# The down projection of an encoder layer: products one by one, and the weights of three of them made ahead

## The reference

```python
def swiglu(h, w_gu, w_down):
    gu = h @ w_gu
    gate, up = jnp.split(gu, 2, axis=-1)
    return (jax.nn.silu(gate) * up) @ w_down

def reference(x, ...):
    for l in range(DEPTH):                      # DEPTH = 2
        ...
        h = rms_norm(x, ffn_norm[l])
        x = x + swiglu(h, w_gu[l], w_down[l])
```

## Time and profile before

| | us |
|---|---|
| median of 3 runs (2769.6 to 2775.0) | 2771.93 |
| the profiled execution | 2774.79 |
| its span, first to last instruction | 2773.1 |
| layer 1: down projection, first to last start of a matmul | 1170.08 to 1387.59 |
| layer 2: the same | 2538.91 to 2756.43 |

### The profile page before, as it was taken

How to read it: one execution, slowest core, us unless ns; L and a number is a source line. 1 busy time by engine, 2 the same in 40 slices (tenths; PEclk the granted TensorE clock), 3 DMA queues, 4 the chain that set the end, 5 groups by cost and what they waited for, 6 DMA issues and landing times. The chain is left out here.

```text
span 2773.1 us, 37893 instructions
## 1 busy us (share of the span) xinstructions
PE 2623.2 (95%) x12976; PEld 2166.9 (78%) x12976; DVE 1706.1 (62%) x3334; ACT 1065.6 (38%) x2098; POOL 562.0 (20%) x521
## 2 busy tenths in 40 slices
PE   5999999989799999999979999999897999999997
PEld 5877788777588888878878778878785888888786
DVE  4277657663555555589943766666717555556897
ACT  3222655553522222334342226555515322223342
POOL 2000221110044544300000003111001545442000
PEclk9999999999999999999999999999999999999999
DMA  5211610004122221432232116000222222216123
GB/s 165 79 42 38 146 45 13 18 13 137 61 84 79 89 84 46 142 155 76 76 120 70 39 39 155 28 18 12 88 62 76 91 77 92 76 46 233 51 92 118
DMA packets 230942, 219.84 MB, mean 79 GB/s; under 512 B 54768, under 2 KB 191984, under 8 KB 230768
## 3 DMA queue, kind: packets, MB, share of 16 engines
q1 hardware_dynamic: 222864, 217.61, 24.7%
q10 hardware_dynamic: 7904, 0.04, 0.2%
HBM read 171.87 MB, written 45.73 MB: 78 GB/s over the span
## 5 line engine op out<-in xcount | busy, mean ns | idle before, releaser
L1984 PE MATMUL psum<-OPH_t,WH 128*128 128x512 f32 x704 | 274.5, 390 | 6.7 <-DVE WL L1529 4.8
L1984 PE MATMUL psum<-OPH_t,WL 128*128 128x512 f32 x704 | 273.9, 389 | 0.0
L1984 PE MATMUL psum<-OPL_t,WH 128*128 128x512 f32 x704 | 273.9, 389 | 0.0
L1529 DVE TENSOR_TENSOR WL<-RAW,WH 128x512 fp32r<-128x512 f32 x132 | 160.9, 1219 | 157.0 <-ACT WH L1073 157.0
L958 ACT ACTIVATE T<-T,G 128x192 f32<-128x192 f32 (+4 forms) x352 | 177.3, 504 | 195.4 <-DVE G L1282 191.7
L1792 PE MATMUL psum<-BH,AH 128*128 128x512 f32 x616 | 243.2, 395 | 8.1 <-DVE BL L1597 7.6
L1794 PE MATMUL psum<-BH,AL 128*128 128x512 f32 x616 | 242.4, 394 | 0.0
L1793 PE MATMUL psum<-BL,AH 128*128 128x512 f32 x616 | 242.0, 393 | 0.0
L1984 PE MATMUL psum<-OPH_b,WH 128*128 128x512 f32 x528 | 209.6, 397 | 15.4 <-ACT P1S L1113 9.8
L1882 PE MATMUL psum<-QK,QS 128*128 (+5 forms) x576 | 214.9, 464 | 1.5 <-DVE G L1282 1.5
L1418 DVE COPY PT<-psum 128x256 f32<-128x256 f32 (+3 forms) x254 | 105.5, 415 | 177.9 <-PE psum L1898 176.8
(11 more groups left out here) (193 smaller groups left out, 5668.5 us busy)
## 6 DMA issues: line engine op xcount, KB each, us to landing
RAW<-in_w_gu SPq DMA_DIRECT2D x176, 256.0 KB, 3.8
WDS<-in_w_down SPq DMA_DIRECT2D x88, 256.0 KB, 2.6
UR<-in_w_in SPq DMA_DIRECT2D x56, 256.0 KB, 3.2
g_mid<-GRES SPq DMA_DIRECT2D x28, 512.0 KB, 2.6
WDK<-in_w_down SPq DMA_DIRECT2D x44, 256.0 KB, 6.5
x_res<-X SPq DMA_DIRECT2D x2, 4096.0 KB, 13.7
PR<-in_w_out SPq DMA_DIRECT2D x32, 256.0 KB, 4.2
X<-x_res SPq DMA_DIRECT2D x2, 4096.0 KB, 14.4
```

The source lines that it names most:

```text
L1529: v.tensor_tensor(WL[i][:, :, :], w_source(i, j), WH[i][:, :, :].bitcast(F32), ALU.subtract).then_inc(w_lo, 1)
L1984: last = t.matmul(dst[:, :], w[i][:, k, :], h[o][:, k, :], start=(i in (1, 5, 6) and k == 0 and part == 0), stop=(i in (2, 3, 4) and k == ...
```

## The change

- The seven products run one after the other, in the order 3, 4, 1, 7, 6, 5, 2. In this order consecutive products need few new blocks of gated tiles, and these are fetched as halves (256 KB) when they are needed.
- Products 7 and 6 are accumulated onto the banks of 4 and 1 (no `start` on their first matmul) after those have been added to one target block. X is touched by 40 adds a layer, not 48.
- High and low parts of the weights of products 2, 5 and 7 (33 tiles) are made beside gate/up: SP loads raw tiles (RAWD), POOL makes the sum for product 7 (`part_added`), ACT the high part (`part_high`), DVE the low part (`part_low`), SP sends the pair to DRAM (`w_parts`, 512 KB each). One of them belongs to every fourth product of ORDER. In the down projection the pair is loaded into BR (which holds high and low weights now), three steps ahead. The other four products make their weights in the down projection as before.
- Four gated tiles are kept and 18 sent, not 8 and 14. POOL's list mixes the sums of weights and the gated tiles in another way; SP's list is tied to ORDER.
- `add_product(m)` stands four steps behind the last step of its product; X comes in four pieces of 1 MB.

The core of the diff:

```diff
-            STEPS = [(m, k) for k in range(NK) for m in (2, 5)] + [(m, k) for m in (1, 3, 4, 7, 6) for k in range(NK)]
-            RUNS = [2, 5, 1, 3, 4, 7, 6]
+            RUNS = [3, 4, 1, 7, 6, 5, 2]
+            STEPS = [(m, k) for m in RUNS for k in range(NK)]
+            PARTS = (2, 5, 7)
+            for q in range(len(PARTS) * NK):
+                MADE_BESIDE[16 + 4 * q].append(q)
...
+                    if i == 6:
...
+                        sp.wait_ge(product, DONE[6, NCH - 1])
+                        for k in range(4):
+                            kept_weights(k, 1)
+                        for k in (2, 3):
+                            g_back_in(k, (0, 0))
+                    elif i == 5:
+                        sp.wait_ge(product, DONE[5, NCH - 1])
+                        for k in range(4, 8):
+                            kept_weights(k, 1)
+                    elif i == 2:
+                        sp.wait_ge(product, DONE[2, NCH - 1])
+                        for k in range(8, NK):
+                            kept_weights(k, 1)
+                        for n_ in range(4):
+                            passing_weights(n_)
+                        g_back_in(4, (0, 0))
...
                 sp.wait_ge(g_s, 2 * NCH)
...
+                for n in range(4, len(STEPS)):
                     m, k = STEPS[n]
+                    if n in PASSING:
+                        passing_weights(n)
+                    elif m in PARTS:
+                        sp.wait_ge(step_s, n - 3)
+                        q = 3 * k + PARTS.index(m)
+                        sp.dma_start(BR[:, n % 4, :, :].bitcast(F32), w_parts[q]).then_inc(b_in[n % 4], 16)
+                    if n in (5, 7, 9, 11):
+                        sp.dma_start(X[:, n - 5:n - 3, :], x_res[:, n - 5:n - 3, :]).then_inc(x_again, 16)
+                    if m == 3 and k >= 4:
+                        g_back_in(k, (1, 1))
...
+                def part_low(q):
+
+                    dve.wait_ge(part_hi, q + 1)
+                    v.tensor_tensor(BP[:, q % 2, 1, :], part_source(q), BP[:, q % 2, 0, :].bitcast(F32),
+                                    ALU.subtract).then_inc(part_lo, 1)
...
-                    for m in RUNS[1:]:
-                        if n == LAST_STEP[m] + 3:
+                    for m in RUNS[:-1]:
+                        if n == LAST_STEP[m] + 4:
+                            if m == RUNS[0]:
+                                dve.wait_ge(x_again, 64)
                             add_product(m)
-                add_product(6)
+                add_product(RUNS[-1])
...
                         last = three(bank[BANKS[m][sub]][:, :], AH[:, n % 4, P * sub:P * sub + P], AL[:, n % 4, P * sub:P * sub + P],
-                                     BH[:, n % 4, :], BL[:, n % 4, :], k == 0, k == NK - 1)
+                                     BR[:, n % 4, 0, :], BR[:, n % 4, 1, :], k == 0 and m not in (6, 7),
+                                     k == NK - 1 and m not in (1, 4), skip=True)
```

More of the change, by code:

```diff
@@ new lines, in build_program, with raw_part, part_source @@
+            A_SUMS = running([bool(M[m][0][1]) for m, k in STEPS])
+            B_MADE = running([m not in PARTS for m, k in STEPS])
+            B_SUMS = B_MADE
+            B_LOADED = {n: sum(1 for o in range(n % 4, n + 1, 4) if o not in B_MADE) for n in range(len(STEPS)) if n not in B_MADE}
+            PASSING = sorted(B_SUMS, key=int)
+            PASSING = [n for n in PASSING if STEPS[n][0] != 1]
+            def raw_part(at_):
+                return RAWD[:, at_[0], at_[1], :]
+            def part_source(q):
+                first, sign, second = M[PARTS[q % 3]][1]
+                return BP[:, q % 2, 1, :].bitcast(F32) if sign else raw_part(first)
@@ L620, in g_tile, with g_ready @@
             def g_tile(j, half):
-                t = GRES[:, j % G_KEPT, :] if j >= G_SENT else GLA[:, j, :] if j < 5 else GLB[:, j - 5, :] if j < 13 else GLC[:, 0, :]
+                t = GRES[:, j % G_KEPT, :] if j >= G_SENT else GL[j][:, :]
                 return t[:, 512 * half:512 * half + 512]
+            def g_ready(eng, k, at_):
+                tile_, half = at_
+                if k < 2:
+                    eng.wait_ge(g_s, 2 * PAIRS[k][tile_] + half + 1)
+                else:
+                    eng.wait_ge(g_got[2 * tile_ + half][(k - 2) // 3], 48)
@@ L1643, in _ @@
                         sum_c12(j)
+                    for q in MADE_BESIDE[n - 1]:
+                        part_low(q)
                 step_sum(2)
@@ L1745, in _, with part_added, weight_sums @@
                         mean_powers(fam, b, plan[-1][0]["Q"] + 6)
-                def weight_sums(j):
-                    pool.wait_ge(raw_in[j % 2], 64 * (j // 2 + 1))
+                def part_added(q):
+                    if q % 3 < 2:
+                        return
+                    first, sign, second = M[PARTS[q % 3]][1]
+                    pool.wait_ge(rawd_in, 32 * (q // 3 + 1))
+                    if q >= 2:
+                        pool.wait_ge(part_out[q % 2], 16 * (q // 2))
+                    g.tensor_tensor(BP[:, q % 2, 1, :].bitcast(F32), raw_part(first), raw_part(second), ALU.add).then_inc(part_sum, 1)
+                def weight_sums(j, which=(5, 6, 7, 3)):
+                    if 5 in which:
+                        pool.wait_ge(raw_in[j % 2], 64 * (j // 2 + 1))
                     g0, g1 = RAW[:, j % 2, 0, 0:4, :], RAW[:, j % 2, 0, 4:8, :]
@@ L1753, in weight_sums @@
                                                  (7, g0, u0, ALU.subtract), (3, g1, WS[6][:, :, :], ALU.subtract)):
+                        if i not in which:
+                            continue
                         if j:
```

232 lines of the change are left out of this document (137 added, 95 removed), and 2 rows, old and new, of the table M.

## The result

The changed kernel takes **2784.95 us** (median of 6 runs, 2781.72 to 2789.7) and the kernel before 2772.09 (6 runs): a ratio of 1.0044, 95% interval 1.0031 to 1.0058. It is slower by 12.9 us. The profiled execution of it took 2786.61 us, its span 2784.9. T is again the end of gate/up: 1166.98 in layer 1 of this trace.

The account below looks back on a forecast made before the run. PE bounds gate/up, DVE's adds a stretch of down. Per layer 11.8 us lost at down's start, 8.3 gained, 2.4 tail: net +5.9, +11.8 in both; against the 2771.93 median 2784 us, range 2770 to 2797.

Parts of the forecast that it names:

- Gate/up, 0: Gate/up: making the weights beside it costs 0, bounds 0 to 2 us a layer, because PE sets the pace.
- The 8.3 us at the end of the interleaved products: Down projection: 8.3 us a layer lost while DVE adds finished products; running them one after the other regains it all.
- Tail, +2.4 a layer: End of each layer: eight adds instead of four behind the last matmul, 2.4 us a layer more.
- Step 0, 2.4: First down step: waits for its passing weight tile p0, landing 0.2 us after gate/up ends; 2.4 us lost (1.6 to 3.0).
- Steps 1 and 2, 0.4: Second and third down steps: DVE's nine operations take 5.8 us against PE's 5.4; 0.4 us lost.
- 9 x 0.60: Steps 1 and 2 of down: nine DVE operations at 0.60 us each, plus 0.4, make 5.8 us.
- Step 3, 7.0: Fourth down step: waits for step 4's passing tile p4, 38th load unit, through DVE's list order; 7.0 us lost (5.5 to 8.5).
- The clock, 2.0: Behind step 3's gap in down: PE restarts at half clock, costing 2.0 us more (1.5 to 2.4).
- the queue is quicker: Rival, start of down: loads run at 402 GB/s from the first issue, 6.2 us lost at step 3; about 2776 us; chance 0.18.
- the making isn't covered: Rival, gate/up: each of 33 weight makings holds PE for one DVE operation, 23 us a layer, 2830 us; chance 0.05.
- p4 not behind the backlog: Rival, start of down: step 4's passing tile lands within 9 us of gate/up's end; 2760 to 2765 us; chance 0.09.
- from step 4 on I take 0: Down from step 4: two steps' loads need 5.2 us of 5.4, helped by step 3's gap; 0 us lost.

Follow-up runs that it names:

- e4: Changed kernel with the making of ready weights beside gate/up left out except for the first pair of tiles; 2785.05 us.
- e11: Kernel before the change, with products 2 and 5 run in sequence instead of interleaved, product 2 added six steps later; no ready weights; 2758.2 us.
- e9: e8 with the first four passing weight tiles of product 6 issued earlier, at steps 22 to 25; 2756.87 us.
- e3: Changed kernel with products in the order 3, 4, 2, 7, 1, 5, 6, so the last goes to one tile (four adds, not eight); 2781.77 us.
- e8: e7 with the product order of e10 (3, 1, 2, 6, 4, 5, 7); 2764.63 us.
- e12: e9 with GpSimd multiplying the last gated tile at once again, not after step 3; 2759.66 us.
- e1: Changed kernel with 13 load units of 256 KB moved behind the passing tile of step 4, X issued three steps later; 2792.03 us.
- e6: Changed kernel with 6 load units of 256 KB, not 13, moved behind the passing tile of step 4; 2783.66 us.
- e10: Changed kernel with only the product order exchanged, for 3, 1, 2, 6, 4, 5, 7, and gated-half loads to suit; 2787.45 us.
- e5: e1 with SP's wait for the last gated tile moved from ahead of step 4's loads to step 8's; 2787.14 us.
- e7: Changed kernel with loads in the order the steps need them and GpSimd's last gated-tile multiplications held until after step 3; 2781.2 us.
- e2: Changed kernel with, in steps 3 to 10, DVE's low halves placed ahead of the sum for the next step; 2784.83 us.

## Why the prediction was right, point by point

The forecast, 2784 us, was made for the reasons that the trace shows: the late passing tile, the sum's place in DVE's list, the half clock and the longer tail. That the sum comes within 0.4 us of the loss in either layer is in part luck. Step 0 came out 1.2 to 1.4 us under its term, steps 1 and 2 1.6 over, step 3 1.4 under, the rest 0.6 to 1.5 over. And the largest term is no simple price.

- *Gate/up, 0:* right (377.90 and 378.00 us; e4).
- *The 8.3 us at the end of the interleaved products:* regained in full. e11 shows that sequence alone gives back 6.2 of them, without ready weights and without the new order. That ready weights buy nothing beyond them is borne out by e11, which is as fast as e9 without any; the changed kernel without them was not run.
- *Tail, +2.4 a layer:* 19.10 against 16.67 us; e3, e8 to e12 end in 16.6 to 16.7.
- *Step 0, 2.4:* too much for this trace. 1.0 and 1.2 us were lost. p0, the 14th unit, landed at T - 1.2 and not T + 0.2, so the count taken from the earlier trace rows was 1.4 us late. In the seven other kernels with the same list up to p0 (e1 to e6, e10) the loss is 0.7 to 2.4 us: this term varies from run to run.
- *Steps 1 and 2, 0.4:* too little; 2.0 were lost. The step that failed is "9 x 0.60": it took DVE's operations at the spacing that they have in the earlier trace rows, where GpSimd does nothing. Two of them took 1.7 us beside its multiplications. The sign was there: in the earlier trace rows a subtraction of the same size takes 1.27 us on average in gate/up, where GpSimd is busy for half the time, and the kernel before has low halves of 0.93 and 1.53 us at this very place.
- *Step 3, 7.0:* 5.6 were lost. p4 came at T + 15.1, forecast T + 16.0, and steps 1 and 2 had used up more of the time. Step 3 started at T + 17.2, forecast T + 18.0. e6 gives 0.6 us a unit (3.5 to 3.9 for six), so its cause, the 38th place in the queue, is shown.
- *The clock, 2.0:* what remains of the loss in the two layers, 3.5 and 2.6 us, is the half clock and small pauses. In layer 1, 13 matmuls, and in layer 2, 6 start about 0.43 us apart, 2.6 and 1.2 us more than at full clock, behind the same gap of 5.8 us.

Lost in all, it was 12.1 and 11.4 for a forecast 11.8. Of the rivals, "the queue is quicker" would have needed p4 at T + 12.4, and "the making isn't covered" gaps in gate/up; neither is there. "p4 not behind the backlog" named the point where that gap ends, T + 9.1, but not what follows: in e1 and e5, where the gap is gone, the loss comes later, and no kernel with this order came near its 2760 to 2765. The weak step is "from step 4 on I take 0": by e1, e5 and e6 it held only because the gap at step 3 gave the queue time, as the prediction itself says and did not follow up.

What stays open: why e5 loses as much as it does. From 1174 to 1182 its queue moved only 259 GB/s, while SP's list stood behind the four slots of WDS; more slots were not tried. e8 against e7, which differ in the order alone, shows that what comes second is the cause of the gaps from T + 39 on, and of what its steps need only the passing tiles become fewer: the gated halves are as many, and DVE has four operations a step and not three. Whether they cost by their bytes or by SP's waits for their slots is not shown.

## What to carry to other kernels

When a stage begins with a backlog of loads, count for each step what has to be there by then, not only what stands ahead of the first late tile: taking a load out of the way of one step helps only if the steps behind it can wait for it. A gap may be the time in which a queue catches up, and then removing it moves the loss. Before adding made-ahead operands and a new order, try the smallest edit on the stall that the trace shows: here running two products in sequence, two lines, gave as much as all the rest together.

## What the runs showed of the hardware

- A DVE subtraction of 128x512 from two SBUF tiles that starts while a GpSimd operation of the same shape is under way ends 0.5 to 0.6 us after that operation, whenever it has started. At the start of the down projection it took 0.93 to 1.79 us and not 0.68: GpSimd's multiplication from 1168.68 for 1.59 us ends at 1170.27, DVE's subtraction at 1170.82. In gate/up of the changed kernel's trace 186 subtractions do the same (0.54 to 0.62 us). The Trainium skill, "SBUF — State Buffer", section "SBUF: two separate sides", says that the port pair of the two engines is locked by whichever starts first for its whole instruction, and that a DVE operation with two SBUF inputs counts against a GpSimd operation that reads SBUF, as these do; this trace agrees.
- One queue in steady state moved 387 to 396 GB/s from 1160 to 1192 in the changed kernel and 404 in e11. The Trainium skill, "DMA: Bandwidth & Descriptors", Specifications, has about 358 GB/s as HBM's limit for a core, half of a stack's 716; these runs, with one core at work, lie above it.
- The length of a gap alone did not decide whether the matmuls ran at half clock behind it. After gaps of 5.8 us (changed kernel) and 3.3 us (e2) they did, after gaps of 1.7 us (e6) and 2.6 us (e8) they did not, but in e3 they did after 2.9 us at T + 201 of layer 2, and e1 has a gap of 4.0 us in each layer, behind which the granted clock stays at 1.00 in layer 1 and falls in layer 2. The table by stages of e1 has the rows behind the two gaps:

```profile
1221.00:1225.00 4.00, 3.65 (x16) 3.09 (x17) 3.82 (x7) 2.33 (x5) 0.00 (x0) 1.00 0.55 161
...
2598.00:2602.00 4.00, 4.00 (x11) 3.14 (x12) 3.82 (x7) 1.78 (x3) 0.00 (x0) 0.57 0.60 181
```
